# Rotary angles worked out on GpSimd, and their two sines moved behind the rounding of the fourth weight slab

## What is computed

```python
def rope(x, pos):
    d = x.shape[-1]
    inv = ROPE_THETA ** (-jnp.arange(0, d, 2, dtype=jnp.float32) / d)
    ang = pos.astype(jnp.float32)[..., None] * inv
    cos = jnp.cos(ang)[..., None, :]
    sin = jnp.sin(ang)[..., None, :]
    ...
    return jnp.concatenate([x1 * cos - x2 * sin, x2 * cos + x1 * sin], axis=-1).astype(x.dtype)

def retention_mixer(xn, pos, w_in, gn, w_out):
    ...
    q, k, v, g = jnp.split(xn @ w_in, [H * dk, 2 * H * dk, 2 * H * dk + H * dv], axis=-1)
    q = rope(q.reshape(B, S, H, dk), pos)
    k = rope(k.reshape(B, S, H, dk), pos) * (dk ** -0.5)
```

## Time and profile before

| | us |
|---|---|
| median of 3 runs | 1892.75 |
| lowest and highest of them | 1892.37, 1894.83 |
| span of the profiled execution, first to last instruction | 1892.9 |
| busy: PE / DVE / ACT / POOL | 1694.2 / 1352.8 / 1084.9 / 0.2 |

### The profile page before, as it was taken

How to read it: one execution, slowest core, us unless ns; L and a number is a source line. 1 busy time by engine, 2 the same in 40 slices (tenths; PEclk the granted TensorE clock), 3 DMA queues, 4 the chain that set the end, 5 groups by cost and what they waited for, 6 DMA issues and landing times.

```text
span 1892.9 us, 21567 instructions
## 1 busy us (share of the span) xinstructions
PE 1694.2 (90%) x7672; PEld 1384.0 (73%) x7672; DVE 1352.8 (71%) x1387; ACT 1084.9 (57%) x1089; POOL 0.2 (0%) x4
## 2 busy tenths in 40 slices
PE   6998889997878686799899999998998998999986
PEld 5885768885658565688787787786886886877865
DVE  6645444555438363798898897897997987988964
ACT  5354333344434342676676676675776766766753
POOL 0000000000000000000000000000000000000000
PEclk9999889998888796899999999999999999999998
DMA  5552334553425104599798897897896996987922
GB/s 223 215 181 86 134 113 177 200 184 127 141 101 185 54 25 187 213 373 347 280 368 316 316 374 306 306 378 285 332 375 255 367 377 244 369 337 293 373 109 89
DMA packets 64077, 459.62 MB, mean 243 GB/s; under 512 B 7200, under 2 KB 7200, under 8 KB 8480
## 3 DMA queue, kind: packets, MB, share of 16 engines
q1 hardware_dynamic: 64032, 459.01, 64.5%
HBM read 457.94 MB, written 1.05 MB: 242 GB/s over the span
## 4 chain that ended last, share of the span: by engine, by line
PE 79%; DVE 11%; ACT 5%; issue 3%; DMA 1%; DVEq 0%; ACTq 0%; SPq 0%
PE banks L366 25%; PE banks L368 24%; PE banks L367 24%; DVE weights_low L1062 3%; ACT weights_high L744 2%; PE banks L439 2%; PE banks L414 1%; DMA raw_static<-static_dram 1%; PE banks L691 1%; PE banks L690 1%; DVE activations_t L1084 1%; DVE residual L1497 1%; ACT activations_t L770 1%; DVE scores_t L1385 0%; PE banks L609 0%
## 5 line engine op out<-in xcount | busy, mean ns | idle before, releaser
L1062 DVE TENSOR_TENSOR weights_low<-scratch,weights_high 128x2048 fp32r<-128x2048 f32 x336 | 761.5, 2289 | 114.8 <-ACT weights_high L744 114.7
L744 ACT ACTIVATE weights_high<-scratch 128x2048 fp32r<-128x2048 f32 x336 | 642.6, 1915 | 124.5 <-PE banks L368 124.4
L366 PE MATMUL banks<-weights_high,activations_t 128*128 128x512 f32 (+1 forms) x1568 | 628.3, 401 | 66.0 <-DVE weights_low L1062 49.8
L367 PE MATMUL banks<-weights_low,activations_t 128*128 128x512 f32 (+1 forms) x1568 | 614.2, 392 | 0.0
L368 PE MATMUL banks<-weights_high,activations_t 128*128 128x512 f32 (+1 forms) x1568 | 614.2, 392 | 0.0
L366 PEld LDWEIGHTS banks<-weights_high,activations_t 128*128 128x128 f32 x1568 | 301.7, 192 | 130.8 <-DVE weights_low L1062 32.4
L368 PEld LDWEIGHTS banks<-weights_high,activations_t 128*128 128x128 f32 x1568 | 301.3, 192 | 62.1
L367 PEld LDWEIGHTS banks<-weights_low,activations_t 128*128 128x128 f32 x1568 | 302.4, 193 | 56.6
L1062 DVE TENSOR_TENSOR weights_low<-raw_static,weights_high 128x2048 fp32r<-128x2048 f32 x99 | 221.8, 2257 | 123.3 <-ACT weights_high L744 121.8
L744 ACT ACTIVATE weights_high<-raw_static 128x2048 fp32r<-128x2048 f32 x99 | 185.1, 1892 | 122.6 <-PE banks L368 110.2
L366 PE MATMUL banks<-weights_high,hidden_t 128*128 128x512 f32 x536 | 214.3, 400 | 9.5 <-DVE hidden_t L1236 9.5
(11 more groups left out here) (226 smaller groups left out, 1026.2 us busy)
## 6 DMA issues: line engine op xcount, KB each, us to landing
scratch<-expert_dram SPq DMA_DIRECT2D x336, 1024.0 KB, 5.5
raw_static<-static_dram SPq DMA_DIRECT2D x97, 1024.0 KB, 4.9
consts_sb<-const_dram SPq DMA_DIRECT2D x1, 1058.0 KB, 6.9
residual<-x_dram SPq DMA_DIRECT2D x1, 1024.0 KB, 4.9
out_dram<-residual SPq DMA_DIRECT2D x2, 512.0 KB, 2.8
small_sb<-small_dram SPq DMA_DIRECT2D x1, 704.0 KB, 8.1
raw_static<-static_dram SPq DMA_DIRECT2D x2, 256.0 KB, 3.0
scratch<-gain_dram SPq DMA_DIRECT2D x1, 512.0 KB, 5.7
```

Source lines behind the costliest of these rows:

```text
L366: pe.matmul(oo, xh, wh, start=first, stop=False)
L367: pe.matmul(oo, xh, wl, start=False, stop=False)
L744: A(WH[:, slot, 0:w], raw[:, 0:w], ACT.Copy).then_inc(high_ready, 1)
L1062: V_.tensor_tensor(WL[:, slot, 0:w], raw[:, 0:w], WH[:, slot, 0:w].bitcast(F32), ALU.subtract).then_inc(low_ready, 1)
```

## The change

GpSimd gets a program. It waits for the positions and the constants, casts, multiplies and reduces the angles as DVE did, each step linked by the new semaphore `pool_step`, and signals `ang_done`. Every `scalar_tensor_tensor` of DVE becomes two instructions there, a `tensor_scalar` multiply into a third scratch (in `SG[:, 1, 0:384]`) and a `tensor_tensor` add. DVE loses that work. On ACT the wait for `ang_done` and the two Sin activations move behind `upto(3)` of the loop's first turn, and on DVE the wait for `trig_done` moves behind its `upto(3)`.

```diff
--- before.py
+++ after.py
@@ -263,7 +263,7 @@
         high_ready, low_ready, slab_used = sem("high_ready"), sem("low_ready"), sem("slab_used")
         bank_free = sem("bank_free")
         t_done, t_high, t_low = sem("t_done"), sem("t_high"), sem("t_low")
-        dve_step, hid_step = sem("dve_step"), sem("hid_step")
+        dve_step, pool_step, hid_step = sem("dve_step"), sem("pool_step"), sem("hid_step")
         sq_done, ms_done, rt_done, xn_done = sem("sq_done"), sem("ms_done"), sem("rt_done"), sem("xn_done")
         ang_done, trig_done, gr_high, gr_low = sem("ang_done"), sem("trig_done"), sem("gr_high"), sem("gr_low")
         rope_done, v_done, sig_done, sg_done = sem("rope_done"), sem("v_done"), sem("g_sigmoid"), sem("g_silu")
@@ -799,13 +799,14 @@
             norm_t(0, T_NORM0)
             upto(2)
 
-            act.wait_ge(ang_done, 1)
-            A(SIN[:, :, :], SIN[:, :, :], ACT.Sin)
-            A(COS[:, :, :], COS[:, :, :], ACT.Sin).then_inc(trig_done, 1)
             A(GRH[:, :, :], W[:, W_GR:W_GR + KT * 32].rearrange("p (k n) -> p k n", k=KT), ACT.Copy).then_inc(gr_high, 1)
             for c in range(12):
                 s = A_RIN + 2 * c + 1
                 upto(s + 2)
+                if c == 0:
+                    act.wait_ge(ang_done, 1)
+                    A(SIN[:, :, :], SIN[:, :, :], ACT.Sin)
+                    A(COS[:, :, :], COS[:, :, :], ACT.Sin).then_inc(trig_done, 1)
                 if 4 <= c < 8:
                     act.wait_ge(slab_used, s + 1)
                     for tt in range(NT):
@@ -1045,6 +1046,46 @@
             ple_gate(base, CH_PROJ1, 1)
 
 
+        @block.gpsimd
+        def _(pool):
+            done = [0]
+
+            def plink(ins):
+
+                done[0] += 1
+                ins.then_inc(pool_step, 1)
+                pool.wait_ge(pool_step, done[0])
+
+            pool.wait_ge(pos_in, 16)
+            pool.wait_ge(const_in, 16)
+            plink(nc.gpsimd.tensor_copy(posf, posi[:, 0:3]))
+            c1 = 6.28125
+            c2 = float(np.float32(TWO_PI - c1))
+            c2 = float(np.frombuffer(np.uint32(np.frombuffer(np.float32(c2).tobytes(), np.uint32)[0] & 0xFFFFF000)
+                                     .tobytes(), np.float32)[0])
+            c3 = float(np.float32(TWO_PI - c1 - c2))
+            ang = [TC[:, 0:384].rearrange("p (a n) -> p a n", a=3), TS[:, 0:384].rearrange("p (a n) -> p a n", a=3),
+                   SG[:, 1, 0:384].rearrange("p (a n) -> p a n", a=3)]
+            magic = float(1.5 * 2 ** 23)
+            for a in range(3):
+                m = nc.gpsimd.tensor_scalar(ang[0][:, a, :], cols(C_INV, P), posf[:, a:a + 1], None, ALU.mult)
+            plink(m)
+            for dst, quarter in ((SIN, 0.0), (COS, 0.25)):
+                k_ = ang[1]
+                plink(nc.gpsimd.tensor_scalar(k_, ang[0], float(1 / TWO_PI), quarter, ALU.mult, ALU.add))
+                plink(nc.gpsimd.tensor_scalar(k_, k_, magic, None, ALU.add))
+                plink(nc.gpsimd.tensor_scalar(k_, k_, magic, None, ALU.subtract))
+                plink(nc.gpsimd.tensor_scalar(ang[2], k_, -c1, None, ALU.mult))
+                plink(nc.gpsimd.tensor_tensor(dst[:, :, :], ang[2], ang[0], ALU.add))
+                plink(nc.gpsimd.tensor_scalar(ang[2], k_, -c2, None, ALU.mult))
+                plink(nc.gpsimd.tensor_tensor(dst[:, :, :], ang[2], dst[:, :, :], ALU.add))
+                plink(nc.gpsimd.tensor_scalar(ang[2], k_, -c3, None, ALU.mult))
+                plink(nc.gpsimd.tensor_tensor(dst[:, :, :], ang[2], dst[:, :, :], ALU.add))
+                if quarter:
+                    plink(nc.gpsimd.tensor_scalar(dst[:, :, :], dst[:, :, :], float(np.pi / 2), None, ALU.add))
+                plink(nc.gpsimd.tensor_scalar(dst[:, :, :], dst[:, :, :], 3.1415925, -3.1415925, ALU.min, ALU.max))
+            pool.sem_inc(ang_done, 1)
+
         @block.vector
         def _(dve):
             V_ = nc.vector
@@ -1108,40 +1149,16 @@
             norm_t(0, T_NORM0)
             upto(2)
 
-            dve.wait_ge(pos_in, 16)
-            dve.wait_ge(const_in, 16)
-            link(V_.tensor_copy(posf, posi[:, 0:3]))
-            c1 = 6.28125
-            c2 = float(np.float32(TWO_PI - c1))
-            c2 = float(np.frombuffer(np.uint32(np.frombuffer(np.float32(c2).tobytes(), np.uint32)[0] & 0xFFFFF000)
-                                     .tobytes(), np.float32)[0])
-            c3 = float(np.float32(TWO_PI - c1 - c2))
-            ang = [TC[:, 0:384].rearrange("p (a n) -> p a n", a=3), TS[:, 0:384].rearrange("p (a n) -> p a n", a=3)]
-            magic = float(1.5 * 2 ** 23)
-            for a in range(3):
-                m = V_.tensor_scalar(ang[0][:, a, :], cols(C_INV, P), posf[:, a:a + 1], None, ALU.mult)
-            link(m)
-            for dst, quarter in ((SIN, 0.0), (COS, 0.25)):
-                k_ = ang[1]
-                link(V_.tensor_scalar(k_, ang[0], float(1 / TWO_PI), quarter, ALU.mult, ALU.add))
-                link(V_.tensor_scalar(k_, k_, magic, None, ALU.add))
-                link(V_.tensor_scalar(k_, k_, magic, None, ALU.subtract))
-                link(V_.scalar_tensor_tensor(out=dst[:, :, :], in0=k_, scalar=-c1, in1=ang[0], op0=ALU.mult, op1=ALU.add))
-                link(V_.scalar_tensor_tensor(out=dst[:, :, :], in0=k_, scalar=-c2, in1=dst[:, :, :], op0=ALU.mult, op1=ALU.add))
-                link(V_.scalar_tensor_tensor(out=dst[:, :, :], in0=k_, scalar=-c3, in1=dst[:, :, :], op0=ALU.mult, op1=ALU.add))
-                if quarter:
-                    link(V_.tensor_scalar(dst[:, :, :], dst[:, :, :], float(np.pi / 2), None, ALU.add))
-                link(V_.tensor_scalar(dst[:, :, :], dst[:, :, :], 3.1415925, -3.1415925, ALU.min, ALU.max))
-            dve.sem_inc(ang_done, 1)
             dve.wait_ge(gr_high, 1)
             V_.tensor_tensor(GRL[:, :, :], W[:, W_GR:W_GR + KT * 32].rearrange("p (k n) -> p k n", k=KT),
                              GRH[:, :, :].bitcast(F32), ALU.subtract).then_inc(gr_low, 1)
 
             V_.memset(RT[:, 4096 + 3840:8192].bitcast(F32), 0.0)
-            dve.wait_ge(trig_done, 1)
             for c in range(12):
                 s = A_RIN + 2 * c + 1
                 upto(s + 2)
+                if c == 0:
+                    dve.wait_ge(trig_done, 1)
                 if c < 4:
                     dve.wait_ge(slab_used, s + 1)
                     for tt in range(NT):
```

## The result

| | us |
|---|---|
| before, median of 20 runs (lowest to highest) | 1894.28 (1886.84 to 1900.16) |
| after, median of 20 runs (lowest to highest) | 1899.61 (1894.06 to 1905.16) |
| ratio after to before, 95% interval | 1.0028 (1.0018 to 1.0038) |
| span of the profiled execution, before / after | 1892.9 / 1899.4 |

The kernel got slower by 0.28%, some 5.3 us (3.4 to 7.2 by the interval), where I had forecast no change. The range ended at 1896.8 and didn't hold it. Of the 7.0 us between my 1892.6 and 1899.61, 1.5 are the kernel before itself: its median over 20 runs is 1894.28, not the 1892.75 of the three runs that I had. That profiled execution of the changed kernel took 1901.03 us as a run, 1.6 more than its span.

A forecast was written before the change was run, and what follows sets the result against it. PE, busy 90% of 1892.9 us, was taken as the bound; closing its hole at slab 4 (-0.61) and a later PE start (+0.4) gave -0.2 us on the median 1892.75, so 1892.6, range 1891.2 to 1896.8.

The forecast's parts named there:

- PE's hole of 0.61 us: At slab 4, PE's lateness against an undisturbed slab; 0.61 us, all that the change can win.
- T: Time at which ACT's two sines may start; forecast 35 us, with bounds of 19 and 44.7.
- the chain from T to slab 4: Sines 0.94, `rope` of chunk 0 4.35, `low` of slab 4 2.29, hand-off 0.15: PE starts slab 4 at T + 7.7.
- T = 36.8 for no loss: Latest start of the sines at which slab 4 is undisturbed and the whole 0.61 us is won; break-even is 37.3.
- the covered table load: ACT's Sin table load, 1.28 us, behind `high` of slab 3 from 30.4 to 31.7; covered if T is later than 31.7.
- GpSimd's pace: Time of GpSimd's 25 angle instructions: bounds 10.3 and 25.1 us from DVE's rows, middle 17.7 taken.
- The estimate of 14 us for the 21 large instructions: From the Trainium skill's cycle figures for GpSimd: 15 x 0.58 + 6 x 0.84 us, before hand-offs.
- The stops: GpSimd standing still while DVE runs certain instructions, mainly `low` steps: nothing up to 11 us, 8.7 charged.
- The held start: DVE's early `low` steps wait for GpSimd instructions; PE starts up to 2.4 us later, 1893 to 1894.6; chance 0.14.
- very late angles: Sines from T = 41.1 on delay slab 4, PE may restart slowly; 1896.5 to 1901.8 us; chance 0.14.
- Late angles: GpSimd bounds slab 4; above T = 37.3 each microsecond is lost; chance 0.20 below 0.2%, 0.14 above.
- the case in which the angles are hidden: Forecast case: T under 36.8 and PE's start late by under 1 us; 1892.1 to 1893.1 us; chance 0.48.

The follow-up runs named there:

- late start: Changed kernel with GpSimd's start held until DVE has taken the `low` of slab 2; one run of 1904.76 us, 11.3 over the median before.
- multiply-add: Changed kernel with every 128x384 `tensor_scalar` of GpSimd but the clamp written as multiply and add; median 1893.08 us against 1893.49 before, ratio 0.9996.
- second trace: Profile of the changed kernel run again with no edit; median 1897.46 us against 1892.92 before, ratio 1.0022.
- longer chain: Changed kernel with ten more clamps of the cosine angles at the end of GpSimd's work; ratio to before 1.0052, +9.9 us.

## Why the prediction was wrong, point by point

The frame held: PE's hole of 0.61 us as all that can be won, the chain from T to slab 4 (T + 7.7; measured 7.75 at T = 39.66, 41.24, 41.43, 47.13 and 51.07), T = 36.8 for no loss (none at 35.21, 2.33 at 39.66), `high` of slab 3 at 28.5 (28.22), GpSimd's start at 8.6 (8.50), the covered table load (30.15 to 31.4). What failed is one number, T, and one price behind it, the clock.

**GpSimd's pace, the step that failed.** I took 17.7 us for the 25 instructions, the middle of 10.3 and 25.1. Undisturbed they take 24.9, and T came 6.2 us after my 35. By terms: eleven `tensor_scalar` with one operation, 1.17 to 1.18 each, 12.9 us, where I had set one price of 0.36 to 0.86 for all fifteen, so these lie above my upper bound; four with a multiply-add or the clamp, 0.51, 2.0 us; six `tensor_tensor`, 1.01, 6.1 us (between my 0.56 and 1.29); hand-offs of 0.08 to 0.1, 23 of them 1.9 us; the first four instructions 2.0. The upper end of my range was nearly right and the middle 7.2 too low. That the upper end fits is luck: it had the one-operation form and the first four too cheap, and the multiply-add, the two-input form and the hand-offs too dear. The estimate of 14 us for the 21 large instructions was low as well; they took 21.0. With no row for an operation on an engine, the middle of two bounds was a guess and I let the forecast hang on it with 1.8 us to spare.

**The stops.** I charged 8.7 us. Measured from the durations against those of the late start they are 0.47 + 0.31 + 2.16 + 1.24 + 1.92 + 1.70 = 7.8 us (L1071, L1075, L1078, L1079, L1082, and L1078 of the cosine). The first two ran beside DVE's scaling of x (L1119, 10.14 to 11.58), which has one SBUF tile and a column of scalars as inputs, the other four beside `low` steps. With 24.9 + 7.8 the chain is 32.7 and T = 41.24. Without the stops T would have been 33.4, without the slow form 35.21 as measured (multiply-add): either alone keeps T under 36.8, both together do not. What the Trainium skill (SBUF — State Buffer, Who interferes with whom) states, that a DVE instruction with two inputs in SBUF contends with a GpSimd instruction that reads SBUF, agrees with the four stops beside `low` steps. That each excludes the other for a whole instruction doesn't come out on DVE's side: the `low` of 17.04 began while L1078 (14.55 to 17.88) was still running and took 2.31. In this trace it was GpSimd that paid.

**The held start, a rival that came only in part.** In the profile after, DVE's early `low` steps began as before (14.56 and 17.04, 0.20 behind ACT the second time) and took 2.29 and 2.31; PE began at 20.98, not later. The rest of the gate weights took 0.72 there and in the second trace, against 0.42 before, off the path. In the longer chain, whose first 25 instructions are those of the changed kernel, the same two `low` steps took 2.63 and 3.08, the second beside GpSimd's L1079 (15.73 to 17.97), and PE began at 21.75, 0.8 us later. So the mechanism exists and some executions of the changed kernel may have it; how many isn't known. I had put 0.4 us on it in the forecast and 0.14 of chance.

**The price of being late.** The rival "very late angles" is what happened, at its very edge, T = 41.24 against the 41.1 that I had set for it. But I had set that point with no clock in it, kept the clock for gaps beyond, and sized it there as four slow matmuls, 1.6 us. In the profile after, the gap of 4.56 us brought 2.7 us of it, 13 slow steps, so that 3.94 became 6.65; behind the gap of 3.29 there was none. The runs say +5.3 and +4.5 us, between the two. By my sum without the clock, T = 41.24 gives 1892.75 + 3.94 = 1896.7, just inside the range. What took the median of 1899.61 out of it is 1.4 us more than 3.94, which would fit a lower clock behind the gap in some executions and not in others (argued, not shown), and the 1.5 us by which the kernel before stands higher than its first three runs. The range should have reached 1901.8, the upper end that I had worked out and then cut off with 0.14.

**The chances.** Late angles, below and above 0.2%, together had 0.34; given that the sum rested on an unpriced engine, a middle of T = 35 with ends at 19 and 44.7 was no reason for 0.48 on the case in which the angles are hidden.

**Left open:** when the clock falls. In one trace each it stayed full at gaps of 1.35 and 3.29 us and was lower behind those of 4.56, 5.08, 9.18 and 14.04; from PE's start behind the gap to the end of slab 4 that cost 2.7, 2.5, 2.3 and 1.6 us, so it didn't grow with the gap. Why one operation takes GpSimd longer than a multiply-add wasn't tried beyond the forms above.

## What to carry to other kernels

Before work is moved to an idle engine, work out the latest time at which it may end (here T = 36.8) and price each instruction form on that engine from a trace of it, not from the engine that did it before; where no such trace is at hand, forecast from the slow end. A multiply-add with a neutral constant (x 1.0, or + 0.0) in place of a single operation took this chain's dearest form on GpSimd from 1.17 to 0.51 us. Work on GpSimd beside DVE must be priced with its stops. And a wait of PE can cost more than its length: behind four of them, of 4.56 to 14.04 us, the lower clock added 1.6 to 2.7 us here.

## What the runs showed of the hardware

On GpSimd, 128x384 f32 in SBUF: `tensor_scalar` with multiply-add or min-max 0.51 us, with one operation (add, subtract or multiply) 1.17 to 1.18, with add-add or subtract-add 1.50; `tensor_tensor` add 1.01. While DVE ran a `tensor_tensor` of 128x2048 with both inputs in SBUF (2.29 us), GpSimd's instruction was longer by 1.2 to 2.3 us over the traces; beside DVE's instructions that read PSUM and one SBUF tile it was not. DVE's instruction took 2.29 to 2.31 in the changed kernel's first trace, but 2.63 and 3.08 in that of the longer chain. The granted clock fell while PE stood idle (0.74 in a window without a matmul). It differs between executions of one kernel: the two traces of the changed kernel have 0.89 and 0.96 in the same 80 us, with 295 and 315 matmuls.
